# Three projection units instead of two over each block of a norm, in a one-core float32 trunk

## What is computed

```python
for l in range(DEPTH):
    h = modulate(rms_norm(x, norm_mix_g[l]), sh1, sc1)
    y = stick_window_mixer(h, ...) if l % 2 == 0 else hgrn2_mixer(h, ...)
    x = x + g1[:, None, :] * y
    h = modulate(rms_norm(x, norm_ffn_g[l]), sh2, sc2)
    x = x + g2[:, None, :] * conv_ffn(h, ...)
return rms_norm(x, final_g)

def conv_ffn(h, w_gate, w_up, conv_w, conv_b, w_down):
    a = causal_dwconv3(h @ w_gate) + conv_b          # along the sequence, per channel
    return (gelu(a) * (h @ w_up)) @ w_down           # D_FF = 2816

def hgrn2_mixer(h, w_in, lb, onorm_g, w_out):
    q, fr, i, g = split(h @ w_in)                    # 8 heads of 128 channels
    log_f = log(lb + (1 - lb) * sigmoid(fr)); k = 1 - exp(log_f)
    o = hgrn2_recurrence(q, k, i, log_f)             # needs the running sum of log_f
    return (rms_norm(o, onorm_g) * silu(g)) @ w_out
```

## Time and profile before

| | |
|---|---|
| median of 3 runs | 1300.44 us (1299.4 to 1300.88) |
| profiled execution: its own time | 1300.57 us |
| its span, first to last instruction | 1298.8 us |
| PE busy | 1262.1 us (97%), 7071 matmuls |
| DVE busy | 818.4 us (63%) |
| ACT busy | 554.8 us (43%) |
| mean granted TensorE clock | 0.997 of 2.4 GHz |

### The profile page before, as it was taken

The page is one execution under the profiler, slowest core; times in us unless marked ns, Lnnn a source line. Parts: engine busy times, 40 slices in busy tenths (PEclk is TensorE's granted clock), DMA queues, the critical chain, the costliest instruction groups (busy, mean ns, idle before and its releaser), DMA issues.

```text
span 1298.8 us, 18991 instructions
## 1 busy us (share of the span) xinstructions
PE 1262.1 (97%) x7071; PEld 1021.7 (79%) x7071; DVE 818.4 (63%) x1191; ACT 554.8 (43%) x837; POOL 46.8 (4%) x92
## 2 busy tenths in 40 slices
PE   6999998999999999999999999999999999999997
PEld 5777777868888888878778888888688888888786
DVE  5776667676666666556787887776855555552423
ACT  7665556343333333121356655653433333331212
POOL 1000000000000000001000000001000000000000
PEclk9999999999999999999999999999999999999999
DMA  9644520535445454556513222226233333332232
GB/s 331 196 130 146 163 81 2 163 97 162 145 142 146 134 154 145 172 160 226 184 55 94 66 82 74 78 78 210 66 102 96 96 95 97 97 97 97 92 103 81
DMA packets 190074, 160.09 MB, mean 123 GB/s; under 512 B 5271, under 2 KB 163176, under 8 KB 190018
## 3 DMA queue, kind: packets, MB, share of 16 engines
q1 hardware_dynamic: 177696, 116.34, 29.7%
q0 software_dynamic: 11776, 42.29, 10.8%
q10 hardware_dynamic: 546, 0.69, 0.1%
HBM read 157.20 MB, written 2.10 MB: 123 GB/s over the span
## 4 chain that ended last, share of the span: by engine, by line
PE 88%; DVE 5%; SPq 2%; ACT 2%; issue 1%; DMA 1%; DVEq 0%; ACTq 0%
PE proj L1684 62%; PE z L1684 21%; PE obank L1684 3%; PE misc L1684 1%; SPq L512 1%; SPq L522 1%; DVE normed L1106 1%; DVE hT_lo L1112 1%; ACT w_hi L654 1%; DMA w_raw<-ab_w_in 1%; DVE w_lo L1068 0%; DVE xT L1491 0%; PE z L2244 0%; ACT hT_hi L686 0%; PE misc L1957 0%
## 5 line engine op out<-in xcount | busy, mean ns | idle before, releaser
L1684 PE MATMUL proj<-hT_hi,w_hi 128*128 128x512 f32 x1112 | 439.6, 396 | 1.1 <-ACT hT_hi L686 0.9
L1684 PE MATMUL proj<-hT_lo,w_hi 128*128 128x512 f32 x1112 | 434.6, 391 | 2.9 <-DVE hT_lo L1112 2.9
L1068 DVE TENSOR_TENSOR w_lo<-w_raw,w_hi 128x1024 fp32r<-128x1024 f32 x189 | 231.1, 1224 | 321.4 <-ACT w_hi L654 321.3
L1684 PE MATMUL proj<-hT_hi,w_lo 128*128 128x512 f32 x1112 | 433.2, 390 | 0.0
L654 ACT ACTIVATE w_hi<-w_raw 128x1024 fp32r<-128x1024 f32 x191 | 201.9, 1058 | 404.0 <-PE proj L1684 230.9
L1684 PEld LDWEIGHTS proj<-hT_lo,w_hi 128*128 128x128 f32 x1112 | 208.8, 188 | 52.4 <-DVE hT_lo L1112 9.3
L1684 PEld LDWEIGHTS proj<-hT_hi,w_hi 128*128 128x128 f32 x1112 | 208.8, 188 | 50.3 <-issue 8.7
L1684 PEld LDWEIGHTS proj<-hT_hi,w_lo 128*128 128x128 f32 x1112 | 208.7, 188 | 44.2
L1684 PE MATMUL z<-gated_hi,w_hi 128*128 (+1 forms) x264 | 103.6, 392 | 2.7 <-DVE xT L1491 2.7
L1684 PE MATMUL z<-gated_hi,w_lo 128*128 (+1 forms) x264 | 103.1, 390 | 0.0
L1684 PE MATMUL z<-gated_lo,w_hi 128*128 (+1 forms) x264 | 103.0, 390 | 0.0
(11 more groups left out here) (342 smaller groups left out, 1485.5 us busy)
## 6 DMA issues: line engine op xcount, KB each, us to landing
ada_raw<-ada_w POOLq DMA_DIRECT2D x80, 512.0 KB, 4.2
w_raw<-ffn_w_gate SPq DMA_DIRECT2D x44, 512.0 KB, 3.8
w_raw<-ffn_w_up SPq DMA_DIRECT2D x44, 512.0 KB, 3.8
w_raw<-ffn_w_down SPq DMA_DIRECT2D x44, 512.0 KB, 3.3
w_raw<-hg_w_in SPq DMA_DIRECT2D x32, 512.0 KB, 4.1
ada_first<-ada_w SPq DMA_DIRECT2D x16, 512.0 KB, 11.0
w_raw<-ab_w_in SPq DMA_DIRECT2D x14, 512.0 KB, 4.0
w_raw<-ab_w_out SPq DMA_DIRECT2D x8, 512.0 KB, 4.2
```

The costliest lines, as they stand in the source:

```text
L1068: nc.vector.tensor_tensor(w_lo[:, slot, :], w_raw[:, slot, :], w_hi[:, slot, :].bitcast(F32), ALU.subtract).then_inc(lo_done, 1)
L1684: return nc.tensor.matmul(dst, weights_ap, moving, start=start, stop=stop, skip_group_check=True)
```

## The change

`unit_triple` takes the place of `unit_pair` behind norms 1, 2 and 3. The third unit writes the bank `zb[0]`. The first unit's split weights lie in parts of buffers that are free there (`gated_hi` and `gated_lo` blocks, or `oT_hi` and `oT_lo`), so the second and third have the two slots. The order of the triple at norms 1 and 3 is, for blocks 0 to 5, second, first and third unit, and then blocks 6 and 7 of the second, of the first, of the third. At norm 2 the second and first unit run together, two blocks of the third stand between their blocks 4 and 6, and its other six behind them.

At norms 1 and 3 all three units are split ahead of `root` and `normalise`. At norm 2 the third is split on ACT behind `hT_hi` of block 3 and on DVE behind `hT_lo` of block 3. The fourth unit (`split_behind`) is split when the triple's first finished unit is through. The halved splits remain only at the output projections, where `unit_pair` stays.

```diff
@@ -122,7 +122,12 @@
-PAIRS = [U_OUT0, U_FFN0, U_IN1, U_OUT1, U_FFN1]
+PAIRS = [U_OUT0, U_OUT1]
+TRIPLES = [U_FFN0, U_IN1, U_FFN1]
+TRIPLE_ORDER = [[(k, s) for k in range(6) for s in (1, 0, 2)] + [(k, s) for s in (1, 0, 2) for k in (6, 7)]] * 3
+THIRD_BEHIND = 4
+TRIPLE_ORDER[1] = ([(k, s) for k in range(4) for s in (1, 0)] + [(4, 1), (4, 0), (0, 2), (5, 1), (5, 0), (1, 2)]
+                   + [(k, s) for s in (1, 0) for k in (6, 7)] + [(k, 2) for k in range(2, 8)])
@@ -282,6 +287,10 @@
+        extra_hi = [t.rearrange("p a n -> p (a n)") for t in
+                    (gated_hi[0][:, 18:20, :], oT_hi[:, 6:8, :], gated_hi[1][:, 18:20, :])]
+        extra_lo = [t.rearrange("p a n -> p (a n)") for t in
+                    (gated_lo[0][:, 2:4, :], oT_lo[:, 6:8, :], gated_lo[1][:, 2:4, :])]
@@ -663,6 +672,20 @@
+            def split_triple(u, s):
+
+                i = TRIPLES.index(u)
+                act.wait_ge(raw_in[s % 2], (u + s) * 8 + (48 - 8 * (s % 2)))
+                act.wait_ge(unit_mm, u if i == 1 else u + min(s, 1) - 1)
+                dst = (extra_hi[i], w_hi[:, 1, :], w_hi[:, 0, :])[s]
+                nc.scalar.activation(dst, w_raw[:, s % 2, :], ACT.Copy).then_inc(hi_done, 1)
+
+            def split_behind(u):
+
+                act.wait_ge(raw_in[1], (u + 3) * 8 + 40)
+                act.wait_ge(unit_mm, u + 1)
+                nc.scalar.activation(w_hi[:, 1, :], w_raw[:, 1, :], ACT.Copy).then_inc(hi_done, 1)
+
@@ -685,6 +708,8 @@
                                          bias=shift[:, dc:dc + 1]).then_inc(h_hi, 1)
+                    if n == 2 and dc == THIRD_BEHIND - 1:
+                        split_triple(U_IN1, 2)
@@ -877,10 +902,13 @@
                         split_second(u0 + 2)
+                    elif o < DC - 2:
+                        split(u0 + o + 2, o % 2)
                     elif o < DC - 1:
-                        split(u0 + o + 2, o % 2)
+                        split_triple(u0 + DC, 0)
                     squares(n, o)
-                split(u0 + DC + 1, 1)
+                split_triple(u0 + DC, 1)
+                split_triple(u0 + DC, 2)
                 root(n)
@@ -890,28 +918,29 @@
                     u = u0 + 2 * f
-                    behind_pair = isinstance(f, int)
-                    if behind_pair:
-                        split_first(u + 2)
+                    first = isinstance(f, int) and f == 0
+                    if first:
+                        split_behind(u)
                     else:
...
-                    act.wait_ge(unit_mm, u + 1)
-                    nc.scalar.activation(normed[:, 0, 2:2 + SEQ], proj[0][:], ACT.Copy
+                    act.wait_ge(unit_mm, u + 2 if first else u + 1)
+                    gate = zb[0] if isinstance(f, int) and f == 1 else proj[0]
+                    nc.scalar.activation(normed[:, 0, 2:2 + SEQ], gate[:], ACT.Copy
                                          ).then_inc(proj_free[0], 1)
-                    if behind_pair:
-                        split_second(u + 2)
                     act.wait_ge(conv_done, base + f + 1)
...
                                          bias=conv_col(layer, 3, f)).then_inc(gelu_done, 1)
-                    split(u + 3, 1)
+                    if not first:
+                        split(u + 3, 1)
                     act.wait_ge(gp_done, base + f + 2)
...
                 one(0)
-                with act.Fori(1, FB) as f:
+                one(1)
+                with act.Fori(2, FB) as f:
                     one(f)
@@ -1112,6 +1148,8 @@
                                                        op0=ALU.add, op1=ALU.subtract).then_inc(h_lo, 1)
+                    if n == 2 and dc == THIRD_BEHIND:
+                        split_triple(U_IN1, 2)
@@ -1437,9 +1478,9 @@
                     u = u0 + 2 * f
-                    if isinstance(f, int) and f == 0:
-                        split_first(u + 2)
-                        split_second(u + 2)
+                    first = isinstance(f, int) and f == 0
+                    if first:
+                        split(u + 3, 1)
                     else:
@@ -1572,15 +1614,10 @@
                     gated_head_lo(h - 2)
-                if h == 0:
-                    split_first(u + 2)
                 if h < HG_HEADS:
-                    dve.wait_ge(unit_mm, u + 1)
+                    dve.wait_ge(unit_mm, u + 1 if h else u + 2)
                     nc.vector.tensor_scalar(f_tile, proj[0][:], CLAMP, None, ALU.min).then_inc(f_clamped, 1)
-                    if h:
-                        split(u + 2, 0)
-                    else:
-                        split_second(u + 2)
+                    split(u + 2 if h else u + 3, 0 if h else 1)
                 if h:
@@ -1748,6 +1783,26 @@
+            def unit_triple(u, h_from):
+
+
+                i = TRIPLES.index(u)
+                banks = (proj[0], proj[1], zb[0])
+                his = (extra_hi[i], w_hi[:, 1, :], w_hi[:, 0, :])
+                los = (extra_lo[i], w_lo[:, 1, :], w_lo[:, 0, :])
+                for k, s in TRIPLE_ORDER[i]:
+                    if k == 0:
+                        pe.wait_ge(hi_done, u + s + 1)
+                        pe.wait_ge(lo_done, u + s + 1 - len(QUAD))
+                    at = slice(k * P, (k + 1) * P)
+                    pe.wait_ge(h_hi, h_from + k + 1)
+                    mm(banks[s][:], his[s][:, at], hT_hi[:, k, :], start=(k == 0))
+                    mm(banks[s][:], los[s][:, at], hT_hi[:, k, :])
+                    pe.wait_ge(h_lo, h_from + k + 1)
+                    last = mm(banks[s][:], his[s][:, at], hT_lo[:, k, :], stop=(k == DC - 1))
+                    if k == DC - 1:
+                        last.then_inc(unit_mm, 1)
+
@@ -2048,11 +2103,12 @@
                 pe.wait_ge(gp_done, base + 1)
-                unit_pair(u0, h_from)
+                unit_triple(u0, h_from)
                 def one(f):
-                    pe.wait_ge(proj_free[0], FREE0_FFN[layer] + f)
-                    unit(u0 + 2 * f, 0, proj[0][:])
+                    if not (isinstance(f, int) and f == 1):
+                        pe.wait_ge(proj_free[0], FREE0_FFN[layer] + f)
+                        unit(u0 + 2 * f, 0, proj[0][:])
@@ -2228,8 +2284,9 @@
                     head_values(p)
-                pe.wait_ge(f_clamped, h + 1)
-                unit(u + 2, 0, proj[0][:])
+                if h:
+                    pe.wait_ge(f_clamped, h + 1)
+                    unit(u + 2, 0, proj[0][:])
                 if h:
```

More of the change, by code:

```diff
@@ L934, in down @@
                 if not last:
-                    split(u0 + FB, 0)
-                    split(u0 + FB + 1, 1)
+                    split_triple(u0 + FB, 0)
+                    split_triple(u0 + FB, 1)
                     root(n)
@@ L1030, in _ @@
                         act.wait_ge(hvt_full, h)
-                    nc.scalar.activation(vT1[:], proj[0][:], ACT.Copy).then_inc(hv_ready, 1)
+                    values = proj[0] if h else zb[0]
+                    nc.scalar.activation(vT1[:], values[:], ACT.Copy).then_inc(hv_ready, 1)
                 if h:
@@ L1085, in split_second, with split_triple @@
                                         w_hi[:, 0, HALF_UNIT:].bitcast(F32), ALU.subtract).then_inc(lo_done, 1)
+            def split_triple(u, s):
+                i = TRIPLES.index(u)
+                dve.wait_ge(hi_done, u + s + 1)
+                lo = (extra_lo[i], w_lo[:, 1, :], w_lo[:, 0, :])[s]
+                hi = (extra_hi[i], w_hi[:, 1, :], w_hi[:, 0, :])[s]
+                nc.vector.tensor_tensor(lo, w_raw[:, s % 2, :], hi.bitcast(F32), ALU.subtract).then_inc(lo_done, 1)
             def add_squares(n, dc):
@@ L2222, in _ @@
                 if h == 0:
-                    unit_pair(u, h_base["norm2"])
+                    unit_triple(u, h_base["norm2"])
                 else:
```

## The result

The changed kernel takes 1312.53 us in the median of 4 runs (1311.12 to 1313.73), beside 1300.56 us of the kernel before (4 runs): ratio 1.0093, 95% interval 1.0080 to 1.0106. It is 12.0 us slower; 9.9 had been forecast, and the time lies just above the range that ended at 1312.5. Run again in a later study it took 1311.93 us, beside 1300.13, ratio 1.0091 (1.0077 to 1.0106).

What follows compares the result with a forecast made beforehand. PE was 88% of the chain of waits, so its waits and issue were taken to set the end. Delays of 2.2 + 1.5 + 2.8 = 6.5 plus 3.4 for the clock made 9.9 over 1300.4: 1310.3 us, range 1306.0 to 1312.5.

Steps and rivals of the forecast that it cites:

- norm 1, delay without clock: Norm 1 and feed-forward 0: the fourth unit, waiting for the product that frees `proj[1]`, starts 2.2 us later.
- norm 2, head 0: Norm 2: clamp 2.4 us later, 0.9 regained behind `k_hg`, so head 0's running sum and what follows come 1.5 us later.
- norm 3, delay without clock: Norm 3 and feed-forward 1: late third-unit load and the wait for the product together cost 2.8 us.
- clock on the path: Clock falls behind the two new 3.2 us waits ahead of the fourth units, 1.7 us each, 3.4 us together.
- What bounds it: Whole kernel: 88% of the chain of waits is PE, so the end moves only with what PE waits for or issues.
- the wait behind it: Ahead of the fourth unit in feed-forward 0: PE idles 3.2 us for the product that frees `proj[1]`.
- The rival that the product comes in time: Feed-forward stages: `proj[1]` is free when the triple ends; 2.45 us faster in all, 1298.0 us; chance of faster 0.05.
- The late norms: Norms 1 and 3: the third unit's split ahead of the root makes them start 0.8 and 1.35 us later.
- The term that 0.9 comes back behind `k_hg`: Head 0 at norm 2: 0.9 us of the clamp's 2.4 us delay is regained before the running sum.
- the fall of the clock behind it costs nothing: Behind the wait at head 0's fourth unit: what follows has over a microsecond of slack to DVE's scores, so 0 us.
- a rival of 0.11: Norm 3: 2.2 us of idle time ahead of the triple brings a third clock fall, 1.7 us more, 1312.0 us; chance 0.11.
- One wait taken for a price: Trace of before: PE idle 2.69 us, then granted clock 0.57 over 4 us, read as a loss of 1.7 us.

Runs made afterwards that it cites:

- after: The changed kernel, with the triple at norms 1, 2 and 3, against the kernel before, and its profiled execution; 1312.53 us, ratio 1.0093.
- norm 2 only: The changed kernel with the triple at norm 2 alone, norms 1 and 3 keeping the pair; 1302.24 us, ratio 1.0016 to the kernel before.
- norm 3 only: The changed kernel with the triple at norm 3 alone, norms 1 and 2 keeping the pair; 1307.16 us, ratio 1.0055 to the kernel before.
- four idle matmuls at norm 3: The changed kernel with four idle matmuls in place of two behind the sum of norm 3; 1309.61 us, ratio 1.0071 to the kernel before.

## Why the forecast was right in its sign and too low

| term | forecast | measured | from |
|---|---|---|---|
| norm 1, delay without clock | 2.2 | 0.75 + 3.28 - 1.72 = 2.3 | after |
| norm 2, head 0 | 1.5 | 1.83 | norm 2 only |
| norm 3, delay without clock | 2.8 | 1.34 + 4.81 - 3.44 = 2.7 | after, norm 3 only |
| clock on the path | 3.4 (two falls) | 5.2 (three falls) | after |
| sum | 9.9 | 12.0 | |

That the measured column adds up to the difference of the medians to a tenth is in part luck: the two profiled spans differ by 11.7 us, and single terms come from different executions.

- **What bounds it** was right: the new waits, not the busy time, set the end. The triple itself gained what the rows said, the wait behind it is 3.27 and 3.34 us where 3.2 was forecast, and it took the place of the old ones. The rival that the product comes in time has nothing for it.
- **The late norms** came to 0.75 (forecast 0.8) and 1.34 (1.35).
- **Norm 2** was mis-sized: the norm starts at 648.74 (645.23 before), so the clamp comes 15.90 us behind it (13.19 before), 2.71 later and not 2.4 (2.48 by the forecast's own starts, 660.9 and 658.42), and the running sum 19.81 (17.99), 1.82 later and not 1.5. Block 4's rest was ready when it was forecast, 9.1 us behind the norm's start; what was too short is the way from there to the clamp, 6.76 us against 6.5. The term that 0.9 comes back behind `k_hg` held. The wait for `vT` behind head 0's fourth unit is 2.76 us, and that the fall of the clock behind it costs nothing held.
- **The failed step is the count of the clock's falls.** The prediction took "two new waits of 3.2 us ... 1.7 each" and left the idle time at norm 3 aside as a rival of 0.11, "shorter than the 2.69 that is shown". It had worked out the 2.2 us of idle time itself (2.27 measured), and it gave that wait no fall because the only one it looked at was longer. The runs show in its place a third fall that costs 1.63 us: behind 2.15 to 2.27 us of idle time at norm 3 the clock fell in 4 profiled executions of 4, and in the kernel before behind 2.80 and 1.75 (one execution each). The price was right: 1.72 us a fall, in nearly every case. The trace of before has a shorter wait too, which the forecast did not look at, 2.46 us at 216.85, and behind it the clock held at 1.00; the same wait in the changed kernel, at 214.84, is followed by a fall (windows of before, then of after):

```profile
216.85 0.98 PE L1919 MATMUL proj<-table,q_sb 128*128 128x128 f32 x7 [2.46 <-DVE q_sb L1309]
216.00:220.00 4.00, 3.15 (x37) 2.74 (x38) 2.86 (x12) 2.33 (x8) 0.00 (x0) 1.00 0.02 4
214.84 1.54 PE L1974 MATMUL proj<-table,q_sb 128*128 128x128 f32 x6 [2.46 <-DVE q_sb L1347]
216.00:220.00 4.00, 4.00 (x35) 3.36 (x34) 3.22 (x9) 1.60 (x4) 0.00 (x0) 0.72 0.02 4
```

So one trace could not have settled it: the row at hand would have spoken for the forecast, and it takes several executions to see that the clock falls behind such waits more often than not. The Trainium skill, page "TensorE: Matmul & The Clock Gate", section "HAM oscillation — how this bites in real kernels", has waits of some 3 to 5 us between bursts put the clock to half. The runs agree in most cases and not in all, since the 3.35 us wait at 949.10 of "four idle matmuls at norm 3" left it at 1.00, and they show the fall behind shorter waits too. The rival's 1312.0 is the time that was measured, less the 0.3 at norm 2 and roundings.

- **One wait taken for a price** was read too quickly. The fall behind the 2.69 us wait at 579.75 gave the forecast its 1.7. In lost clock that is right, in time it is not: from there to norm 2's first matmul takes 67.1 us with the fall (9 executions) and 66.8 without (5), since PE has slack behind. The new waits had none, so the figure held where it was used.

## What to carry to other kernels

A change that fills waits also spends the slack that hides other things: before it is made, list what has been late inside those waits (a bank to be freed, a chain behind the first unit, a fall of the clock) and price each of them without cover. Price an idle time of PE as its length and, where nothing behind it has slack, one fall of the clock (1.7 us here), also where idle time only grows by a microsecond, as here from 0.9 to 2.2 us. And give the unit that follows the triple a bank of its own before the units are packed closer: here that took 8.1 us back.

## What the runs showed of the hardware

A fall of the clock has a fixed size here, but the same wait does not bring it in every execution. Over the 14 profiled executions (without their last 10 us) the windows sum to 1.68 to 1.72 us a fall, and to 3.40 to 3.44 in three cases. Behind waits of 3.3 us in the feed-forward stages it fell in 7 of 8 cases, behind 2.8 us ahead of the transposes of head 0 in 4 of 6, behind 2.7 us in `down` in 9 of 14, behind the 2.46 us at about 215 in 8 of 14, and never where the kernel left PE idle for 0.5 to 0.9 us at the norms. What decides between two executions of one kernel is not shown; it was not tried.

The times of the kernel before fall into two groups, 26 of its 68 runs in the three studies at 1298.4 to 1299.3 us and 42 at 1299.9 to 1301.8, with a mean clock of 0.996 to 0.999 and 0.994 to 0.997. The medians of the two groups are 1.5 us apart, about one fall. The profiled executions show where it can come from. PE's first matmul behind norm 1, less the 0.75 of the late norm where there is one, starts at 270.6 to 270.9 us in the five executions that have no fall between 30 and 270 us, and at 271.8 to 273.9 in the nine that have one there, eight of them behind the 2.46 us wait. That the two groups of the kernel before differ by this fall is not shown, since it was profiled once (1300.57 us, with a fall at 44). So the scatter of a kernel that is quoted as a measurement's uncertainty can be a fall that comes or not, and a median of few runs can sit on either step.
